# Gates of 16,384 experts gathered through a DRAM table instead of one-hot matrix products

## What is computed

```python
def one_block(xb):                                   # 128 tokens
    q = jnp.einsum('td,dhk->thk', xb, w_q).reshape(128, 8, 2, 64)
    s = jnp.einsum('thpc,hpnc->thpn', q, sub_keys)
    s1, i1 = lax.top_k(s[:, :, 0], 16)
    s2, i2 = lax.top_k(s[:, :, 1], 16)
    cand_s = s1[..., :, None] + s2[..., None, :]     # 16 x 16 per head
    cand_i = i1[..., :, None] * 128 + i2[..., None, :]
    top_s, pos = lax.top_k(cand_s, 16)
    expert = jnp.take_along_axis(cand_i, pos, axis=-1)
    g = jax.nn.softmax(top_s, axis=-1)
    a = jax.nn.gelu(jnp.einsum('thkd,td->thk', u_emb[expert], xb))
    return jnp.einsum('thk,thkd->td', g * a, v_emb[expert])
```

## Time and profile before

| | |
|---|---|
| median of 3 executions | 3246.32 us (3245.1 to 3246.91) |
| profiled execution, its span | 3243.7 us (no separate time of its own is given) |
| PE busy | 3231.8 us (100%) |
| DVE, ACT, POOL busy | 2175.6, 1675.9, 118.0 us |
| DMA | 594.21 MB, mean 183 GB/s, queue 1 busy 56.6% of 16 engines |
| granted TensorE clock | full (2.4 GHz) in all 40 slices but the small ends |

### The profile page before, as it was taken

One profiled execution on the slowest core, in us unless ns is written; L12 is line 12 of the kernel. 1 busy time (PEld: TensorE's weight loads), 2 busy tenths in 40 slices (PEclk: granted clock), 3 DMA queues, 4 the chain that ended last, 5 costly groups with the idle time before them and its releaser, 6 DMA issues.

```text
span 3243.7 us, 60193 instructions
## 1 busy us (share of the span) xinstructions
PE 3231.8 (100%) x24752; PEld 3088.7 (95%) x24752; DVE 2175.6 (67%) x3677; ACT 1675.9 (52%) x2630; POOL 118.0 (4%) x159
## 2 busy tenths in 40 slices
PE   9999999999999999999999999999999999999998
PEld 9999999999999999999999999999999988888887
DVE  7987486666664486665765898888655555556665
ACT  5556454444444455544555444667544444445545
POOL 0000200000001000000000000222000000000000
PEclk9999999999999999999999999999999999999999
DMA  6444555555566656455666566544565556666555
GB/s 223 150 144 142 178 170 193 187 191 190 189 192 193 193 177 202 139 162 171 190 195 213 182 195 192 167 150 150 169 191 194 193 191 194 194 206 221 193 194 169
DMA packets 168801, 594.21 MB, mean 183 GB/s; under 512 B 19696, under 2 KB 21968, under 8 KB 168400
## 3 DMA queue, kind: packets, MB, share of 16 engines
q1 hardware_dynamic: 168528, 590.36, 56.6%
HBM read 584.55 MB, written 4.19 MB: 182 GB/s over the span
## 4 chain that ended last, share of the span: by engine, by line
PE 98%; DVE 1%; ACT 0%; issue 0%; POOL 0%; DVEq 0%; ACTq 0%; POOLq 0%
PE ps L907 31%; PE ps L908 31%; PE ps L909 31%; PE ps L1349 2%; PE ps L914 1%; PE ps L962 0%; DVE wl L1442 0%; PE ps L934 0%; PE ps L1157 0%; PE ps L1180 0%; PE ps L1177 0%; PE ps L1363 0%; PE ps L1191 0%; PE ps L1181 0%; PE ps L1015 0%; PE ps L964 0%
## 5 line engine op out<-in xcount | busy, mean ns | idle before, releaser
L2210 ACT CAST wh<-raw 128x1024 fp32r<-128x1024 f32 (+2 forms) x1118 | 1160.7, 1038 | 1225.3 <-PE ps L909 1223.5
L1442 DVE TENSOR_TENSOR wl<-raw,wh 128x1024 fp32r<-128x1024 f32 (+2 forms) x1118 | 1348.1, 1207 | 508.3 <-ACT wh L2210 505.4
L907 PE MATMUL ps<-xh,wh 128*128 128x256 f32 x3088 | 863.1, 280 | 0.8 <-ACT vm L2503 0.7
L909 PE MATMUL ps<-xh,wl 128*128 128x256 f32 x3088 | 852.3, 276 | 0.0
L908 PE MATMUL ps<-xl,wh 128*128 128x256 f32 x3088 | 851.9, 276 | 0.0
L907 PE MATMUL ps<-xw,wh 128*128 128x258 f32 (+2 forms) x2096 | 592.3, 283 | 0.1
L909 PE MATMUL ps<-xw,wl 128*128 128x258 f32 (+2 forms) x2096 | 587.6, 280 | 0.0
L907 PEld LDWEIGHTS ps<-xh,wh 128*128 128x128 f32 x3088 | 580.3, 188 | 5.3 <-ACT vm L2503 1.1
L908 PEld LDWEIGHTS ps<-xl,wh 128*128 128x128 f32 x3088 | 580.4, 188 | 1.6
L909 PEld LDWEIGHTS ps<-xh,wl 128*128 128x128 f32 x3088 | 579.8, 188 | 0.0
L908 PE MATMUL ps<-xw,wh 128*128 128x258 f32 (+2 forms) x1441 | 404.5, 281 | 0.0
(11 more groups left out here) (417 smaller groups left out, 4371.1 us busy)
## 6 DMA issues: line engine op xcount, KB each, us to landing
raw<-in_peer_u SPq DMA_DIRECT2D x256, 512.0 KB, 4.3
raw<-in_peer_v SPq DMA_DIRECT2D x256, 512.0 KB, 4.5
raw<-in_w_in SPq DMA_DIRECT2D x172, 512.0 KB, 3.7
raw<-in_w_up SPq DMA_DIRECT2D x82, 512.0 KB, 4.4
raw<-in_w_gate SPq DMA_DIRECT2D x80, 512.0 KB, 4.3
raw<-in_w_down SPq DMA_DIRECT2D x80, 512.0 KB, 4.0
raw<-in_w_out SPq DMA_DIRECT2D x64, 512.0 KB, 4.1
raw<-in_w_branch_a SPq DMA_DIRECT2D x16, 512.0 KB, 3.5
```

What stands on the lines that cost most here:

```text
L907: t.matmul(o, lh, rh, start=start, stop=False)
L909: return t.matmul(o, ll, rh, start=False, stop=stop)
L1442: v.tensor_tensor(part_at(wl, i), raw[:, i % RN, 0:cols(i)], part_at(wh, i).bitcast(F32), ALU.subtract).then_inc(lo, 1)
L2210: s.copy(part_at(wh, i), raw[:, i % RN, 0:cols(i)]).then_inc(hi, 1)
```

## The change

The gates are written into a table in DRAM, one float for each (expert, token), 16.8 MB. POOL adds them with 256 indexed accumulating transfers, each of 128 floats, one per partition (a token). For such transfers the program sets aside `dynamic_dma_scratch_size=1024` bytes per partition, a value that stood there before, when POOL made none. Each of the eight heads of a half waits until the former head's 16 transfers have landed, since two heads may choose the same expert. SP zeroes the table beforehand with 32 transfers of 512 KB during the first block's gate and up products, and reads it back as one 128 x 256 tile per V tile of the first half. DVE multiplies the tile into `G` (`times_gate`). The one-hot steps, their matmuls, `pick` and all that read PSUM for them are gone. All U tiles now come before all V tiles.

```diff
-PLAN += [("U", j, c) for j in range(JB) for c in range(2)]
-for _j in range(JB, 128):
-    PLAN += [("U", _j, 0), ("U", _j, 1), ("V", _j - JB, 0)]
-PLAN += [("V", j, 0) for j in range(128 - JB, 128)]
-PLAN += [("V", j, 1) for j in range(128)]
+PLAN += [("U", j, c) for j in range(128) for c in range(2)]
+PLAN += [("V", j, c) for c in range(2) for j in range(128)]
...
+NZERO, ZERO_AT = 32, [GU + 14 + 5 * n for n in range(32)]
...
+    table = nc.dram_tensor("table", (128 * 128 * S, 1), F32).ap()
...
     # SP
+            if i in ZERO_AT:
+                y.wait_ge(zeroed, 1)
+                y.dma_start(table_zero[ZERO_AT.index(i)], zeros).then_inc(d_zero, 16)
+            if PLAN[i][0] == "V" and PLAN[i][2] == 0:
+                n = PLAN[i][1]
+                if n == 0:
+                    y.wait_ge(d_put[0], 16 * 128)
+                    y.wait_ge(d_put[1], 16 * 128)
+                if n >= 4:
+                    y.wait_ge(coef, n - 3)
+                y.dma_start(gt[n % 4], table_tile[n]).then_inc(d_gt[n % 4], 16)
...
     # DVE
+        def index_3(q):
+
+            after(own.n)
+            v.scalar_tensor_tensor(sel[:, 1, :], sel[:, 0, :], 128.0, sel[:, 1, :], ALU.mult, ALU.add).then_inc(own.up(), 1)
+            after(own.n)
+            v.tensor_scalar(eidx[:, q, :], sel[:, 1, :], float(S), iota[:, 16 + q:17 + q], ALU.mult, ALU.add).then_inc(idx_ok, 1)
...
-            v.tensor_tensor(held(j) if DONE[j] else G[:, j, :], u_place(j), r2, ALU.mult).then_inc(ev_u, 1)
+            v.tensor_tensor(G[:, j, :], u_place(j), r2, ALU.mult).then_inc(ev_u, 1)
...
+        def times_gate(j):
             v.wait_ge(gelu, j + 1)
-            v.wait_ge(g_a, DONE[j])
-            v.tensor_tensor(G[:, j, 0:n], G[:, j, 0:n], held(j)[:, 0:n], ALU.mult).then_inc(coef, 1)
+            v.wait_ge(d_gt[j % 4], 16 * (j // 4 + 1))
+            v.tensor_tensor(G[:, j, :], G[:, j, :], gt[j % 4], ALU.mult).then_inc(coef, 1)
...
     # ACT, before the down products of the first block reuse the tile of zeros
+            if base and m == 0:
+                s.wait_ge(d_zero, 16 * NZERO)
...
     # POOL
+        g.wait_ge(rs, RMS.index("post1") + 1)
+        g.memset(zeros, 0.0).then_inc(zeroed, 1)
...
+        def put(q, head):
+
+            if head:
+                g.wait_ge(d_put[q], 16 * 16 * head)
+            for n in range(16 * head, 16 * head + 16):
+                g.indirect_dma_start(out=table, out_offset=bass.IndirectOffsetOnAxis(ap=eidx[:, q, n:n + 1], axis=0),
+                                     in_=wts[:, q, n:n + 1], in_offset=None, compute_op=ALU.add).then_inc(d_put[q], 16)
+
+        g.wait_ge(d_zero, 16 * NZERO)
+        for q in range(2):
+            g.wait_ge(idx_ok, q + 1)
+            for head in range(8):
+                put(q, head)
```

More of the change, by code:

```diff
@@ L97, in _sides3 @@
             work += [("place", (q, i, 0), 2.6), ("place", (q, i, 1), 2.3), ("place", (q, i, 2), 2.2)]
+        work += [("index", q, 0.4)]
     at[0].append(("sim", 0))
@@ L114, in _sides3 @@
         behind += us
[L115 to L129, removed]
+    return at, slot
+SIDES3, LAST_CHOICE = _sides3()
 UNITS = [("d", h) for h in range(DIF)] + [("f", h) for h in range(FOX)]
@@ L520, in build @@
     spill = nc.dram_tensor("spill", (128, 2, D), F32).ap()
+    table = nc.dram_tensor("table", (128 * 128 * S, 1), F32).ap()
+    table_zero = table.rearrange("(n p c) o -> n p (c o)", n=NZERO, p=128)
+    table_tile = table.rearrange("(j p t) o -> j p (t o)", j=128, p=128)
+    loose = tmp[:].rearrange("p a t -> p (a t)")
+    zeros = loose[:, 0:CH]
+    gt = [loose[:, S * n:S * n + S] for n in range(4)]
+    wts = loose[:, 4 * S:5 * S].rearrange("p (q n) -> p q n", q=2)
+    eidx = loose[:, 5 * S:6 * S].bitcast(U32).rearrange("p (q n) -> p q n", q=2)
     r2 = rstd[:, 0:S]
@@ L630, in carve @@
         carved[0] -= n
-        assert carved[0] >= UEND.index(2 * JH - 1) * S
+        assert carved[0] >= S * sum(e + 1 <= LAST_CHOICE for e in UEND)
         a = flatG[:, carved[0]:carved[0] + n]
@@ L655, in build @@
     gsum = carve(8)
[L657 to L662, removed]
     fin = flatG[:, 0:2 * D].rearrange("p (q d) -> p q d", q=2)
@@ L732, in build @@
     gsig, ev_b, mg_z, mg_h, mg_l, res2 = [new(n) for n in ("gsig", "ev_b", "mg_z", "mg_h", "mg_l", "res2")]
[L734 to L737, removed]
+    qp_ok, x2_t, x2, sim, sim_a, soft_v, soft_a, place_ok, idx_ok = [
+        new(n) for n in ("qp", "x2_t", "x2", "sim", "sim_a", "soft_v", "soft_a", "place", "idx")]
+    ev_u, gelu, coef, c_h, c_l = [new(n) for n in ("ev_u", "gelu", "coef", "c_h", "c_l")]
+    zeroed, d_zero = new("zeroed"), new("d_zero")
+    d_put = [new(f"d_put{q}") for q in range(2)]
+    d_gt = [new(f"d_gt{n}") for n in range(4)]
     v_part, f_add, f_sq, f_ms, f_rt, f_rs, f_out, f_outv = [
@@ L1334, in _ @@
                 by_token(m)
[L1337 to L1349, removed]
         def side_3(name, a):
@@ L1366, in side_3 @@
                         last.then_inc(sim, 1)
[L1367 to L1376, removed]
         def v_part_of(j, half, a):
@@ L1389, in v_tile @@
             t.wait_ge(c_l, n + 1)
[L1390 to L1394, removed]
+            if n == 0:
+                t.wait_ge(sim_a, 8)
+            if n == 128:
+                t.wait_ge(ev_u, 128)
+            for a in range(4):
                 last = v_part_of(j, half, a)
@@ L2060, in soft_3 @@
             after(own.n)
-            v.tensor_tensor(gw, gw, gsum.unsqueeze(2).to_broadcast([128, 8, 16]), ALU.mult).then_inc(own.up(), 1)
+            v.tensor_tensor(wts[:, q, :].rearrange("p (h s) -> p h s", h=8), gw, gsum.unsqueeze(2).to_broadcast([128, 8, 16]),
+                            ALU.mult).then_inc(own.up(), 1)
         def place_3(q, i, part):
@@ L2117, in side_3 @@
                 place_3(*a)
[L2118 to L2124, removed]
+            elif name == "index":
+                index_3(a)
         def read_u(j):
@@ L2148, in _ @@
                 read_u(UAT[slot])
-            if slot - 1 in UAT and DONE[UAT[slot - 1]]:
-                times_G(UAT[slot - 1])
             for name, a in SIDES3[slot]:
                 side_3(name, a)
+            if PLAN[i + 2][0] == "V" and PLAN[i + 2][2] == 0:
+                times_gate(PLAN[i + 2][1])
             if PLAN[i + 1][0] == "V":
@@ L2557, in side_3 @@
                 s.activation(gw, gw, ACT.Exp).then_inc(soft_a, 1)
[L2558 to L2568, removed]
-                        s.activation(one, one, ACT.Relu, bias=ones[:, 0:1], scale=-1.0).then_inc(one_a, 1)
-            elif name == "hot_read":
-                pv = ps[5 + a % 3][:].rearrange("p (t i) -> p i t", t=4)
-                s.wait_ge(g_v, a + 1)
-                s.copy(G[:, TILES_DONE[a]:, 4 * a:4 * a + 4], pv[:, TILES_DONE[a]:, :]).then_inc(g_a, 1)
         def activation(j):
-            n = 4 * DONE[j]
-            z = tmp[:, 3 + j % 3, 0:S] if n else G[:, j, :]
             s.wait_ge(ev_u, j + 1)
-            if n and n < S:
-                s.activation(G[:, j, n:], z[:, n:], ACT.Gelu)
-                s.activation(z[:, 0:n], z[:, 0:n], ACT.Gelu).then_inc(gelu, 1)
-            else:
-                s.activation(z, z, ACT.Gelu).then_inc(gelu, 1)
+            s.activation(G[:, j, :], G[:, j, :], ACT.Gelu).then_inc(gelu, 1)
         def coef_high(n):
             j = n % 128
-            if n == 0:
-                s.wait_ge(g_v, 64)
             if n == 255:
@@ L2592, in coef_high @@
                 s.wait_ge(gemm, AT["V", (n - 2) % 128, (n - 2) // 128] + 1)
-            if n < 128 and j >= JH:
-                s.wait_ge(coef, j - JH + 1)
+            if n < 128:
+                s.wait_ge(coef, n + 1)
             s.copy(coef_at(0, n), G[:, j, :]).then_inc(c_h, 1)
@@ L2695, in _ @@
         g.memset(kpe[64:128, 0, :], 0.0).then_inc(s_const, 1)
-        g.wait_ge(pick, 2)
-        for tk in range(S):
-            if WHO[tk % 8] == "P":
-                if tk >= NHOT:
-                    g.wait_ge(hot_mm, tk - NHOT + 1)
-                g.tensor_scalar(hots[tk % NHOT][0], iota[:], picked[0][:, tk:tk + 1], None, ALU.is_equal).then_inc(one_g, 1)
+        def put(q, head):
[9 more added lines that the diff above has]
+                put(q, head)
     px.close()
@@ L2785, in layouts @@
     A["ident"] = np.eye(128, dtype=np.float32)
-    A["iota"] = np.ascontiguousarray(np.broadcast_to(np.arange(128, dtype=np.float32), (128, 128)))
+    places = np.zeros((128, 18), np.float32)
+    places[:, 0:16] = np.arange(16)
+    places[:, 16] = np.arange(128)
+    places[:, 17] = np.arange(128, 256)
+    A["iota"] = places
     r = np.arange(128)
```

35 lines of the change are left out of this document (1 added, 34 removed).

## The result

The changed kernel takes **3507.53 us** (median of 4 executions, 3506.08 to 3509.23) against 3246.32 for the kernel before: 1.0806 times as long [1.0793, 1.0818], 261 us more. The forecast was 3184 us with a range to 3260, so it was wrong on the other side of zero. What happened is rival (a). One execution of the kernel before (18623.06 us) and one of experiment 6 (8314.67 us), both from the same round, lie far outside the others and are left out of what follows.

A forecast was written before the change was run, and what follows sets the result against it. PE was taken as the bound, busy 3231.8 of 3243.7 us. From 3246.3, 62.8 us of removed PE time came off, all other work and transfers cost 0, and 0.5 was added for small losses: 3184 us, range 3178 to 3260.

The forecast's parts named there:

- rival (a): SP's wait before the first V load: transfers come too late, PE stands once; 3399 us at 3.0 each; chance 0.21 + 0.07.
- PE time removed, 62.8 us: PE's last stage: 64 one-hot groups at 0.94 us give 60.2, plus 2.2 and 0.4 from two smaller stretches.
- The alternation and the first `pick`: Stretch where U and V chunks alternate, 2.2 us saved; stretch with the first `pick`, 0.4 us saved.
- DVE, ACT, `times_gate`: Work removed from DVE and ACT is worth 0; two `index` at 0.5 us and `times_gate` at 0.42 us stay hidden.
- SP's new traffic, 0 us: Zero writes and table reads beside chunk loads raise the DMA share to 0.70 and 0.75, costing PE nothing.
- The deadline, 2465.8 us, or 2.16 us per transfer: First V load must be issued by then, leaving 552 us for 256 transfers, all waits included.
- The price of a transfer: POOL's accumulating transfers: 1.5 us each plus 16 drains of 3.5, 440 us, ending 113 us before the deadline.
- The choice within the bounds: 256 transfers take at least 84 us by issue, 973 if serial; 1.5 us each chosen from POOL's ordinary instructions.
- The 2.0 us fixed per transfer of the Trainium skill: POOL's transfers, strictly serial at that price: 512 us, end at 2425, the same forecast sum.
- its price list: Late transfers before the first V load: slower from 2.40 us each; 3399 us at 3.0, 3604 us at 3.8.
- Rival (b): Beside the transfers, DVE or chunk loads are slowed and PE waits; 3190 to 3230 us; chance 0.09.
- Every chunk 2.72 us: PE's U and V chunks late in the kernel each take 2.72 us, the pace under the whole sum.

The follow-up runs named there:

- experiment 6: Changed kernel with the table for tokens 0 to 127 only, one-hot products for tokens 128 to 255; 3214.31 to 3234.67 us in two groups, ratio 0.9933.
- Experiment 1: Changed kernel without its 256 accumulating transfers, zeroing and table reads kept, SP waiting only for the indices; 3183.83 us, ratio 0.9808.
- experiments 2: Changed kernel with only the first half's 128 transfers (tokens 0 to 127) and a wait only for them; 3183.59 us, ratio 0.9808.
- experiments 3 to 6: The first two: changed kernel with 1152 bytes of scratch, 3459.91 us; with 2048 and shortened `wh` and `wl` rows, 3384.08 us. The last two have their own lines.
- 7 and 8: Changed kernel with work added in PE's gap: 200 dummy DVE subtractions, 3548.66 us; or 100 more chunk loads on SP, 3569.26 us.
- experiment 5: Kernel without the accumulating transfers, SP waiting instead for 600 POOL memsets before the first V load; 3371.82 to 3392.1 us in two groups.

## Why the prediction was wrong, step by step

- **PE time removed, 62.8 us**: right. Experiment 1 gave 3183.83 against the 3184 forecast. The alternation and the first `pick` are too small to be seen singly.
- **DVE, ACT, `times_gate`**: right. `times_gate` takes 418 ns, as assumed, and waited for nothing after the gap. `index` took 0.3 us for each of its two instructions; the indices were ready at 1914 and 2045 us, within a microsecond of the forecast.
- **SP's new traffic, 0 us**: right. The share was 0.68 beside the zero writes (0.70 forecast) and 0.73 in the first V half (0.75), with PE busy throughout.
- **The deadline, 2465.8 us, or 2.16 us per transfer**: right. The last cast before the gap starts at 2468.6, the 256th U chunk's.
- **The price of a transfer**: this step failed. I took 1.5 us each and 3.5 us for each of 16 drains, 440 us. It was 850.7 us, 3.32 each. POOL's own time was 461.0 us: 1.80 in the mean, not 1.5. The pauses of 0.3 us make some 41 us more. The drains were cheaper than assumed, 38.7 us in all. The rest, some 309 us in 103 stops after every third and every seventh transfer, I priced at nothing, and it alone is more than the 113 us of slack that the sum had left.
- **The choice within the bounds**: I had named both ends, 84 and 973 us, and then took the row nearest in kind, POOL's ordinary instructions. A transfer by POOL is not such an instruction. Its price, 3.32 us, lies nearer the upper end, the 3.8 us worked out from the landing of a tiny transfer. And the argument against rival (a), "sixteen are issued without a wait between them", read the program's waits as if they were all; there are 103 more that kernel.py writes nowhere, and 34 of them where the scratch is 2048 bytes.
- **The 2.0 us fixed per transfer of the Trainium skill** (DMA: Bandwidth & Descriptors, Anatomy of one DMA), by which the time would have come out as forecast: measured were 2.59 us from one to the next with all else quiet and 3.94 beside chunks.
- **Rival (a)** had the place and the price list, and named the scratch, with one or two in flight where it was three. Its sign, a POOL row well over 2 us each, did not come: the row says 1.80, and the rest stood in the waits. By its price list 3.32 us per transfer ends the last at 1915 + 850 = 2765 us (measured 2765.8), 300 us after the deadline (PE's gap 299.9). It would give 3184 + 300 = 3484; the other 20 us are the V pace. At 0.28 it had too small a chance: the one unknown of the sum had bounds on both sides of the deadline, and no row showed such a transfer.
- **Rival (b)** had the contention the wrong way round: it is POOL and its transfers that are slowed, and PE never notices.
- **Every chunk 2.72 us**: wrong for the V chunks, 2.80. The size is 20.5 us, and the cause is open.

## What to carry to other kernels

Price a stream of small transfers by POOL by what limits it, the number after which it stops and the time until the newest is done beside the other traffic, and not by the engine's own time alone; and if no row shows such a transfer, give the unknown the chances of its whole range. A wait on the queue that loads everything hands lateness on to the bound engine in full (300 us late, 299.9 of standstill), so ask first how much slack is in front of it: here one half of the transfers fitted (experiments 2 and 6), both did not.

## What the runs showed that was not expected

The slower V pace. PE in the second V half, the kernel before and then the changed one:

```profile
3000.17 0.39 PE L907 MATMUL ps<-wh,ch 128*128 128x512 f32 x1
3000.39 0.39 PE L908 MATMUL ps<-wl,ch 128*128 128x512 f32 x1
3000.62 0.39 PE L909 MATMUL ps<-wh,cl 128*128 128x512 f32 x1
```
```profile
3299.28 0.39 PE L898 MATMUL ps<-wh,ch 128*128 128x512 f32 x1
3299.52 0.39 PE L899 MATMUL ps<-wl,ch 128*128 128x512 f32 x1
3299.75 0.40 PE L900 MATMUL ps<-wh,cl 128*128 128x512 f32 x1
```

Matmuls of 512 columns start 0.227 us apart (2.72/12) or 0.233 us (2.80/12), with the clock granted in full in both. A profile has one pace or the other throughout its V chunks, but for the first and last few matmuls. By their times (each has one profile) the kernel before and experiments 1 and 2 had the faster in every execution; the changed kernel had the slower in all four; experiments 3 to 6 had both; 7 and 8, one execution each, had the slower. POOL's transfers are not needed for it (experiment 5), nor a gap (experiment 6). What selects it stays open. It is worth 20 us in 3200, and it means that a median of a few executions of such a kernel can fall on either side.
